# Two narrow projection units (8 and 16 features) as 32-column stationaries in four quadrants of one PSUM bank, in fp32 from undivided inputs

## What is computed

```
def token_mix(y, w_in, conv_w, conv_b, gate_b, ...):            # first block, "mix"
    p = y @ w_in
    mq, mk, mv, mo, mif, hq, hf, hi, hg = jnp.split(p, PROJ_IDX, axis=-1)
    ...
    gates = (mif + gate_b).transpose(0, 2, 1)                   # mif: 8 features
    log_i, log_f = gates[:, :4], log_sigmoid(gates[:, 4:])
    ...
def gla_mixer(h, w_in, w_a2, b_a, b_r, norm_g, w_o):            # second block, "gla"
    q, k, v, r, a_lr = jnp.split(h @ w_in, [...], axis=-1)      # a_lr: 16 features
    log_a = log_sigmoid(a_lr @ w_a2 + b_a) / 16                 # w_a2: 16 x 512
    ...
    q_dec, k_intra = q * exp(b), k * exp(-b)                    # b: cumsum of log_a in chunks of 64
```

## Time and profile before

| | us |
|---|---|
| median of 3 runs | 2378.87 |
| the profiled execution, device time | 2378.1 |
| its span | 2376.3 |
| granted TensorE clock, mean share | 0.983 |
| TensorE (PE) busy | 2323.5 (98%) |
| VectorE (DVE) busy | 1340.4 (56%) |
| ScalarE (ACT) busy | 835.5 (35%) |

### The profile page before, as it was taken

The page is one execution under the profiler, slowest core; times in us unless marked ns, Lnnn a source line. Parts: engine busy times, 40 slices in busy tenths (PEclk is TensorE's granted clock), DMA queues, the critical chain, the costliest instruction groups (busy, mean ns, idle before and its releaser), DMA issues.

```text
span 2376.3 us, 27553 instructions
## 1 busy us (share of the span) xinstructions
PE 2323.5 (98%) x11130; PEld 1919.8 (81%) x11130; DVE 1340.4 (56%) x1990; ACT 835.5 (35%) x1265; POOL 210.2 (9%) x177
## 2 busy tenths in 40 slices
PE   8999999999999999999999999999999989999998
PEld 6888887877787888888788988888967768888887
DVE  7655548486248455547643576664466664644343
ACT  3322223423434322223633342322344444423221
POOL 0000003021014000003110100000121111000001
PEclk8999999999999999999999999999999999999999
DMA  8766632311212366641332256663131111443331
GB/s 317 248 203 203 198 120 73 111 37 45 62 54 71 101 196 211 202 132 45 108 98 62 63 158 222 208 211 123 37 119 54 54 41 57 150 125 98 97 98 36
DMA packets 81950, 288.07 MB, mean 121 GB/s; under 512 B 9104, under 2 KB 11280, under 8 KB 81824
## 3 DMA queue, kind: packets, MB, share of 16 engines
q1 hardware_dynamic: 81104, 284.74, 37.5%
q10 hardware_dynamic: 720, 1.57, 0.2%
HBM read 284.18 MB, written 2.10 MB: 120 GB/s over the span
## 4 chain that ended last, share of the span: by engine, by line
PE 87%; DVE 8%; ACT 3%; issue 1%; POOL 0%; DMA 0%; SPq 0%; DVEq 0%; ACTq 0%; POOLq 0%
PE bank L280 23%; PE bank L282 23%; PE bank L281 23%; PE bank L472 1%; DVE wlo L1518 1%; PE bank L403 1%; PE bank L404 1%; PE bank L405 1%; PE bank L505 1%; PE bank L429 1%; PE bank L424 1%; PE bank L425 1%; DVE attd L1896 1%; PE bank L316 1%; PE bank L317 1%
## 5 line engine op out<-in xcount | busy, mean ns | idle before, releaser
L1518 DVE TENSOR_TENSOR wlo<-raw,whi 128x1024 fp32r<-128x1024 f32 (+1 forms) x370 | 475.4, 1286 | 342.6 <-ACT whi L948 342.3
L280 PE MATMUL bank<-yhi,whi 128*128 128x512 f32 (+1 forms) x1686 | 662.6, 393 | 0.8 <-DVE ylo L1872 0.5
L282 PE MATMUL bank<-yhi,wlo 128*128 128x512 f32 (+1 forms) x1686 | 651.9, 387 | 0.0
L281 PE MATMUL bank<-ylo,whi 128*128 128x512 f32 (+1 forms) x1686 | 651.9, 387 | 0.0
L948 ACT ACTIVATE whi<-raw 128x1024 fp32r<-128x1024 f32 (+1 forms) x370 | 385.2, 1042 | 304.6 <-PE bank L282 247.3
L280 PEld LDWEIGHTS bank<-yhi,whi 128*128 128x128 f32 x1686 | 318.2, 189 | 82.1 <-issue 16.8
L282 PEld LDWEIGHTS bank<-yhi,wlo 128*128 128x128 f32 x1686 | 317.7, 188 | 64.9
L281 PEld LDWEIGHTS bank<-ylo,whi 128*128 128x128 f32 x1686 | 318.3, 189 | 62.0 <-issue 1.0
L280 PE MATMUL bank<-mlp_ahi,whi 128*128 128x512 f32 (+1 forms) x552 | 206.6, 374 | 0.0
L281 PE MATMUL bank<-mlp_alo,whi 128*128 128x512 f32 (+1 forms) x552 | 206.2, 374 | 0.0
L282 PE MATMUL bank<-mlp_ahi,wlo 128*128 128x512 f32 (+1 forms) x552 | 206.2, 374 | 0.0
(11 more groups left out here) (334 smaller groups left out, 2857.0 us busy)
## 6 DMA issues: line engine op xcount, KB each, us to landing
raw<-in_ada SPq DMA_DIRECT2D x152, 512.0 KB, 4.4
raw<-in_ffn_up SPq DMA_DIRECT2D x88, 512.0 KB, 4.4
raw<-in_mlp_up SPq DMA_DIRECT2D x64, 512.0 KB, 3.6
raw<-in_mlp_dn SPq DMA_DIRECT2D x64, 512.0 KB, 3.6
raw<-in_ffn_dn SPq DMA_DIRECT2D x32, 512.0 KB, 4.2
raw<-in_w_dqkv SPq DMA_DIRECT2D x24, 512.0 KB, 3.6
first<-in_ada SPq DMA_DIRECT2D x16, 512.0 KB, 15.1
raw<-in_ffn_dn SPq DMA_DIRECT2D x16, 384.0 KB, 3.7
```

The lines of the kernel that those rows point to most:

```text
L280: e.matmul(out, wh, xh, start=first, stop=False)
L281: e.matmul(out, wh, xl, start=False, stop=False)
L282: mm = e.matmul(out, wl, xh, start=False, stop=last)
L1518: e.tensor_tensor(k.wlo[:, what % NW, 0:width], raw[:, 0:width], k.f(k.whi[:, what % NW, 0:width]), ALU.subtract).then_inc(*sig.up("wlo", ...
```

## The change

The weights of `mif` and `ga` are laid out as eight blocks of 128 x 32 (128 KB in place of 512 KB a unit). They are neither rounded nor split: TensorE multiplies `raw` by the whole y, both fp32, in the new function `quadrants`: block kt goes to the output partitions 32q to 32q+31 with q = kt modulo 4, so each quadrant of the bank gets two of the eight blocks. `prenorm` gets a function `whole` that adds the shift to `tm(n)` in place once `ylo` has been made of it: eight more ScalarE instructions in each of the two stages.

`four` now makes four `hq` (four `gq`), and the narrow unit follows. Its `raw` slot is held until its last matmul. In `mix` ScalarE copies the whole bank to `tm(3)`, TensorE does one unit `hf`, then adds up the quadrants by one fp32 matmul with 8 stationary columns, and the bias is added to that. In `gla` the quadrants are not added up: `w_a2` is laid out in four copies with zeros between, so `gz` contracts over 128 rows; each `gz` now stands behind its `gk` unit instead of ahead of it. The load of `w_a2` (256 KB in place of 32 KB) is issued by ScalarE. The lines of the diff without their context, but for the hunk that names `w_mif`'s layout:

```diff
@@ -35,8 +35,10 @@
-IDENT, ONES, PERM, CAUS, CNEG, INVF_C, EPS_C, HPI_C, SEL_C, NCONST = 0, 128, 256, 384, 512, 640, 641, 642, 643, 647
-MIX_ORDER = [("mif", 0, 1), ("hq", 0, 4), ("hf", 0, 4), ("hi", 0, 4)]
+IDENT, ONES, PERM, CAUS, CNEG, INVF_C, EPS_C, HPI_C, SEL_C, QUAD_C, NCONST = 0, 128, 256, 384, 512, 640, 641, 642, 643, 647, 655
+QUADRANTS = ("mif", "ga")
+MIX_ORDER = [("hq", 0, 4), ("mif", 0, 1), ("hf", 0, 4), ("hi", 0, 4)]

...
@@ -70,6 +72,8 @@
+    for m in range(8):
+        c[m::32, QUAD_C + m] = 1.0

...
@@ -197,7 +201,7 @@
-                add_units("w_" + part[0], part[0], part[1], part[2])
+                add_units("w_" + part[0], part[0], part[1], part[2], 256 if part[0] == "mif" else 1024)

...
@@ -206,8 +210,8 @@
-            for part in ("ga", "gq", "gk", "gv", "gr", "go"):
-                add("w_" + part, part)
+            for part in ("gq", "ga", "gk", "gv", "gr", "go"):
+                add("w_" + part, part, 256 if part == "ga" else 1024)

...
@@ -282,6 +286,20 @@
+    def quadrants(self, tag, st):
+        w, k = self.w, self.k
+        u = self.count(tag)
+        out = self.bank("u", u)
+        slot, times = k.slot("lin", u)
+        w.wait_ge(k.s_raw[slot], 16 * times)
+        for kt in range(NT):
+            q = kt % 4
+            w.wait_ge(*self.sig.on("yfull", st, kt))
+            mm = self.e.matmul(out[32 * q:32 * q + 32, :], k.raw[:, slot, 32 * kt:32 * kt + 32], k.tm(kt)[:, 0:S],
+                               start=kt < 4, stop=kt >= 4)
+        mm.then_inc(*self.sig.up("lin", u))

...
@@ -606,9 +624,14 @@
-        self.four(["mif", "hq", "hq", "hq"], y, "yhi", 3, 2)
-        self.linear("hq", y)
-        for _ in range(4):
+        self.four(["hq"] * 4, y, "yhi", 3, 2)
+        self.quadrants("mif", "mix")
+        self.linear("hf", y)
+        out = self.bank("mif")
+        w.wait_ge(*sig.on("gquad"))
+        e.matmul(out[0:8, :], k.cst[:, QUAD_C:QUAD_C + 8], k.tm(3)[:, 0:S], start=True, stop=True).then_inc(
+            *sig.up("gsel", "sum"))
+        for _ in range(3):

...
@@ -734,15 +757,15 @@
-        self.four(["ga", "gq", "gq", "gq"], y, "yhi", 3, 2)
-        self.linear("gq", y)
+        self.four(["gq"] * 4, y, "yhi", 3, 2)
+        self.quadrants("ga", "gla")
+            self.linear("gk", y)
-            e.matmul(out, k.tm(0)[0:16, 128 * i:128 * i + 128], k.tm(1)[0:16, 0:S], start=True,
+            e.matmul(out, k.tm(0)[:, 128 * i:128 * i + 128], k.tm(1)[:, 0:S], start=True,
-            self.linear("gk", y)

...
@@ -940,6 +963,9 @@
+            if k.lin[n][2] in QUADRANTS:
+                self.ready += 1
+                continue

...
@@ -1070,6 +1096,13 @@
+        def whole(n):
+            w.wait_ge(*sig.on("ylo", st, n))
+            self.e.activation(k.tm(n)[:, 0:S], k.tm(n)[:, 0:S], k.ACT.Identity,
+                              bias=k.mod[:, 8 * v_shift + n:8 * v_shift + n + 1]).then_inc(*sig.up("yfull", st, n))

...
@@ -1080,6 +1113,11 @@
+            if st != "ffn2" and n > 1:
+                whole(n - 2)
+        if st != "ffn2":
+            whole(6)
+            whole(7)

...
@@ -1168,12 +1206,7 @@
-        self.four(["mif", "hq", "hq", "hq"])
-        u = self.unit("mif")
-        w.wait_ge(*sig.on("lin", u))
-        w.wait_ge(k.s_par, 16)
-        e.activation(gts[0:8, 0:S], k.banks.at("u", u)[0:8, :], F.Identity,
-                     bias=k.pc("mlstm_gate_b", 0, 1, 8)).then_inc(*sig.up("gts", bank=("u", u)))
+        self.four(["hq"] * 4)

...
@@ -1183,10 +1216,18 @@
+        u = self.unit("mif")
+        w.wait_ge(*sig.on("lin", u))
+        e.activation(k.tm(3)[:, 0:S], k.banks.at("u", u), F.Copy).then_inc(*sig.up("gquad", bank=("u", u)))
+            if i == 0:
+                w.wait_ge(*sig.on("gsel", "sum"))
+                w.wait_ge(k.s_par, 16)
+                e.activation(gts[0:8, 0:S], k.banks.at("mif")[0:8, :], F.Identity,
+                             bias=k.pc("mlstm_gate_b", 0, 1, 8)).then_inc(*sig.up("gts", bank=("mif",)))

...
@@ -1299,16 +1340,16 @@
-        self.four(["ga", "gq", "gq", "gq"])
-        u = self.unit("ga")
-        w.wait_ge(*sig.on("lin", u))
-        e.activation(k.tm(1)[0:16, 0:S], k.banks.at("u", u)[0:16, :], F.Copy).then_inc(
-            *sig.up("galr", bank=("u", u)))
+        self.four(["gq"] * 4)
+        u = self.unit("ga")
+        w.wait_ge(*sig.on("lin", u))
+        e.dma_start(k.tm(0)[:, 0:S], k.dram["a2"]).then_inc(k.s_a2, 16)
+        e.activation(k.tm(1)[:, 0:S], k.banks.at("u", u), F.Copy).then_inc(*sig.up("galr", bank=("u", u)))

...
@@ -1513,6 +1554,8 @@
+                if k.lin[what][2] in QUADRANTS:
+                    continue

...
@@ -1927,8 +1970,8 @@
-        self.four(["mif", "hq", "hq", "hq"])
-        for tag in ("mif", "hq", "hq", "hq", "hq"):
+        self.four(["hq"] * 4)
+        for tag in ("hq", "hq", "hq", "hq", "mif"):

...
@@ -2070,13 +2113,15 @@
-        self.four(["ga", "gq", "gq", "gq"])
+        self.four(["gq"] * 4)
+        for tag in ("gq", "gq", "gq", "gq"):
+            self.unit(tag)
+        u = self.unit("ga")
+        w.wait_ge(*sig.on("lin", u))
-        for tag in ("ga", "gq", "gq", "gq", "gq"):
-            self.unit(tag)

...
@@ -2373,7 +2418,7 @@
-                    w.wait_ge(*sig.on("wlo", what0))
+                    w.wait_ge(*sig.on("lin" if k.lin[what0][2] in QUADRANTS else "wlo", what0))

...
@@ -2385,9 +2430,6 @@
-            if what == k.first["ga"] + NW - 1:
-                w.wait_ge(*sig.on("ylo", "gla", 0))
-                e.dma_start(k.tm(0)[0:16, 0:S], k.dram["a2"]).then_inc(k.s_a2, 16)

...
@@ -2563,6 +2605,11 @@
+def by_quadrant(w):
+    return w.reshape(8, 128, 32).transpose(1, 0, 2).reshape(1, 128, 256)

...
@@ -2586,7 +2633,9 @@
-    d["a2"] = x["gla_w_a2_2"][0]
+    d["a2"] = np.zeros((4, 32, 512), np.float32)
+    d["a2"][:, 0:16] = x["gla_w_a2_2"][0]
+    d["a2"] = d["a2"].reshape(128, 512)

...
@@ -2614,7 +2663,7 @@
-    d["w_ga"] = by_feature(np.concatenate([w[:, 3072:3088], w[:, 0:112]], 1))
+    d["w_ga"] = by_quadrant(np.concatenate([w[:, 3072:3088], w[:, 0:16]], 1))

...
```

More of the change, by code:

```diff
@@ L2603, in lay_out @@
     d["w_mqk"] = by_feature(w[:, 0:1024])
-    d["w_mif"] = by_feature(w[:, 2048:2176])
+    d["w_mif"] = by_quadrant(w[:, 2048:2080])
     d["w_mv"] = by_rows(w[:, 1024:1536])
```

## The result

The changed kernel takes 2395.00 us (median of 6 runs, 2389.57 to 2397.46) against 2380.53 us of the kernel before (6 runs): a ratio of 1.0071, 95% interval 1.0058 to 1.0085. The forecast was 2376.8 us with a range of 2371.5 to 2382.5. It is slower, by over three times what could be told from no change, and the fastest of its runs lies 7 us above the range. The profiled execution took 2392.7 us, its span is 2390.9 against 2376.3 before: 14.6 us more.

The account below looks back on a forecast made before the run. TensorE, busy for 98% of the span, was taken to bound the kernel. Terms of -2.1 us in `mix` and 0.0 in `gla` took the median from 2378.87 to 2376.8 us, range 2371.5 to 2382.5.

Parts of the forecast that it names:

- full overlap: In `quadrants`: four tiles run at once with two fp32 matmuls each, 2.11 us a set including 0.39 overhead.
- the first rival: Quadrants in turn, no overlap: 7.27 us a set, together +8.3 us, 2387.2 us, slower; chance 15%.
- the second: Rival of partial overlap in `quadrants`: 4.3 us a set, +0.1 and +2.2 us, 2381.2 us; chance 8%.
- The sum: In `mix`: adding up the quadrants by one fp32 matmul with 8 columns costs TensorE 1.25 us.
- `mix` is -2.14 for -2.1: Stage `mix`: -5.44 + 2.11 + 1.25 = -2.08 us on TensorE, booked as -2.1, with inputs and weights hidden.
- first chain later: In `gla`: ScalarE's first chain starts 1.9 us later after `four`, because the first `gz` moves back.
- two waits for `wlo`: In `gla`: TensorE waits 2.3 us at the second `gv` unit and 2.5 us at the third.
- net 0.0: Stage `gla`: TensorE's gain of 5.0 us is lost in waits behind ScalarE's chains, giving 0.0 us.
- Its own sum of 27.3 us: In `gla`: TensorE's own need from the end of `four` to the first `gv`, 27.3 us against 32.29 before.
- this rival: The clock: granted clock may fall to 1.2 GHz behind the `gla` waits, 1.7 us lost, 2378.5 us; chance 12%.
- the pace of 5.44 us a unit: TensorE's time for one unit of 24 fp32r matmuls, 0.227 us each, taken from five units without a wait.
- the chance of 0.18 for slower: Whole kernel slower by over 0.2%: 0.18, made of the quadrants-in-turn rival and part of the partial-overlap one.

Follow-up runs that it names:

- e12: Changed kernel with constants of 711 columns (+256 bytes), all eight blocks added up in the first quadrant; ratio 1.0039 to the kernel before.
- e11: Changed kernel at +256 bytes (NCONST 711), with ScalarE making `whi` earlier, between a chain's Ln and last two Exps in `gla`; 2371.95 us, ratio 0.9969 to the kernel before.
- e1: Kernel before with only eight unused columns added to the constants (NCONST 655), moving all tensors behind them 32 bytes; ratio 1.0075.
- e10: Changed kernel with NCONST 711, so everything behind `cst` lies 256 bytes further than in the kernel before; ratio 1.0007 to the kernel before.
- e7: Kernel before with eight unused columns ahead of `whi`: `whi`, `wlo` and all behind move 32 bytes, `yhi` and `ylo` stay; ratio 1.0126.
- e3: Kernel before with a pad of eight columns between `ahi` and `alo`, meant to move `alo` alone by 32 bytes; ratio 1.0056.
- e2: Changed kernel with NCONST 663, so `ahi` and `alo` stand 64 bytes higher than in the kernel before; ratio 1.0012 to the kernel before.
- e9: Changed kernel with NCONST 679, so `ahi` and `alo` stand 128 bytes higher than in the kernel before; ratio 1.0071 to the kernel before.
- e13: Changed kernel at +256 bytes (NCONST 711), with the blocks of `quadrants` in the order 0, 4, 1, 5, 2, 6, 3, 7; 2376.22 us in one run.

## Why the prediction was wrong

The mechanisms that it worked out came true, one by one:
- Quadrants: full overlap. From the end of `four`'s stream to the true start of the next unit's it is 2.05 us (1.85 in the view) for the forecast 2.11. The rule cited from the Trainium skill (TensorE: Matmul & The Clock Gate, Part 3, The mechanism), that a weight load overlaps a matmul in flight only in other row groups, was the ground for e12's time and doesn't hold here: all quadrants use all rows, their matmul records start by fours within 0.02 us, and the loads for the next four run with them (the row below). (The 7.27 us named with it are those of the first rival, not the second.) The Trainium skill (TensorE: Matmul & The Clock Gate, Part 3, Measured speedup vs the span model) has 2.38 times for three column tiles, 0.79 a tile. Four tiles reach 6.98 / 1.85 = 3.8 here, 0.94 a tile.

```profile
434.73 0.16 PEld L300 LDWEIGHTS bank<-tmps,raw 128*32 128x32 f32 x8 [0.35 <-issue]
```

- The sum: 1.15 us for 1.25, about 0.1 ahead of it and 0.2 behind it around the 0.86 of an fp32 matmul. `mix` is -2.14 for -2.1, with no wait on L974 or on `whole`.
- `gla`: first chain later by 1.85 (forecast 1.9), two waits for `wlo` of 1.49 and 2.22 us in the view, 1.8 and 2.5 by starts (2.3 and 2.5), net 0.0 (0.0). The first is shorter because TensorE came to `gv` 0.7 us later, behind the third wait of 0.42 us in the view that the prediction did not have. Its own sum of 27.3 us was right: e11, which has no wait ahead of `gv`, needs 27.3.
- The clock fell behind the waits, for 1.6 us; this rival had 12% and 1.7 us.

What failed is a step that wasn't there. The part on the change went over what each engine issues, and booked nothing for a line of the diff that issues nothing: `NCONST` 647 to 655. The sum thus put the rest of the kernel at nothing: the pace of 5.44 us a unit was left standing for all units, 103 of which are in the down projections. But it depends on where the operands lie as well, and those units went to 5.60 us. The missing term is +16.5 us, some 1 us of it given back by the matmuls of 256 columns, and e1 shows it alone: +16.4 us by the medians. None of the rivals ended on that side for that reason, so the chance of 0.18 for slower had the wrong mechanism behind it: the one it was given for, quadrants in turn, did not happen. With the placement mended (e10), 1.0007 of the first median is 2380.5 us, inside the range and within 0.2%, which had 0.70. The forecast itself, 0.9991 of the time before, lies just below e10's interval of 0.9996 to 1.0018, so it was not met in full even then.

Still open: what collides. The runs show that the places of stationary and moving tiles relative to each other count (e7), that a shift by 256 bytes is as good as none (e10), that 32, 64 and 128 bytes cost 20, 7 and 20 ns a block, and that a neighbour matmul's operand counts (e3). They don't show which memory access waits for which, and larger shifts than 256 bytes were not tried.

## What to carry to other kernels

Price every line of a diff that changes the size of an allocation, also when no instruction reads the new part: compare the addresses of all tiles behind it, and shift operands of matmuls by an amount that was shown to be harmless (here 256 bytes), or allocate what may grow last. e10 shows the first; the second was not run. When time is lost, look at mean lengths and start distances of groups that the change did not touch before looking for a new wait. And a gain on the bounding engine counts only up to the next engine's chain: here 5 us lay ready in `gla`, and 4.4 of them came when ScalarE's gap for the scan was filled.

## What the runs showed of the hardware

- A stream of fp32r matmuls of 128 x 128 by 512 columns goes at 226.7 ns a matmul in the placement of the kernel before and 256 bytes from it (e10), and at 229 to 233 ns in the mean with moving and stationary tiles shifted against each other by 32, 64 or 128 bytes, single kinds between 226 and 238 (e1, e2, e9). The shift of one tile slows its unmoved neighbours in the stream too (e3: `whi ahi` from 227 to 232 ns). The Trainium skill (TensorE: Matmul & The Clock Gate, Part 2, Step-by-step: what each phase is for) says that loading the next weights takes no read bandwidth from the running matmul. That gives no reason to expect what e7 shows, where a shift of the weights took matmuls whose moving tile stayed from 227 to 233 ns; whether the load is what slows them is not shown.
- fp32 matmuls in four column tiles run at once, each tile with its own place in the stream: 16 records in 1.85 us, in either of the two orders tried (e13: 1.88), against 6.98 in one tile (e12).
- Going between tile shapes costs little: about 0.1 us ahead of `quadrants` and of the sum and 0.2 behind.
